# Eight slots of split weights at eight distances past a multiple of 512 bytes: a two-layer encoder on one Trainium2 core

## The chip, the cores and the metric

The kernel runs on one core of a Trainium2 chip. The metric is the device time of one execution in microseconds; the time of the kernel before is the median of two runs, 1114.08 us (1114.03 to 1114.13). The engines of the core go by their short names: PE (TensorE, matmuls; its weight loads are shown apart as PEld), DVE (VectorE), ACT (ScalarE), POOL (GpSimd) and SP (SyncE, which here only issues transfers).

## The reference

A trunk of two layers on an input of 512 tokens by 1024 features, in float32.

- Layer 0: RMSNorm, one projection from 1024 to 2304 columns, split between a short gated convolution (512 wide) and a sliding-window attention (8 query heads, 2 key heads, window 128, ALiBi, a learned sink per head); a norm for each half, one output projection of 1024 by 1024, residual.
- Layer 1: RMSNorm, one projection from 1024 to 1696 columns, split between a spatial gating unit and a latent attention (low-rank queries and keys, a shared rotary key, 8 heads, causal by chunks of 64); norms, an output projection, residual.
- After the mixer of each layer: RMSNorm, a SwiGLU feed-forward of 2816 hidden columns, residual:

```python
h = rmsnorm(x, ffn_norm[layer])
gate, up = jnp.split(h @ w_ffn_in[layer], 2, axis=-1)
x = x + (jax.nn.silu(gate) * up) @ w_ffn_out[layer]
```

## The kernel before, in words

Almost all of the work is products of float32 weights with float32 activations. PE takes them in the format float32r, which keeps fewer bits, so each operand is split: a high part (the value rounded to float32r) and a low part (the value minus its high part, rounded again). Each product is three matmuls that add up in the same stretch of PSUM: high by high, high by low and low by high (`product`, lines 1681 to 1685). The activations are held feature by feature: 128 features on the partitions, 512 tokens along the row.

The weights come in 188 loads. A load is up to 1024 float32 values on each of the 128 partitions (two blocks of 128 input features by 512 columns). It passes three tiles:

1. SP issues the transfer into one of the two slots of `raw`, once the low part of the load two before is made.
2. ACT writes the high part into one of the four slots of `w_hi` (`hi`, line 697), once PE has used the load four before.
3. DVE subtracts and writes the low part into one of the four slots of `w_lo` (`lo`, line 1122).

PE waits for the low part (`ready`) and then works through the load: 2 blocks by 4 tiles of 128 columns, each a product of three matmuls, 24 in all for a full load; load n takes slot n modulo 4. In most stages the 128 by 128 tile of the weights is what PE holds (the stationary operand, fetched by a weight load ahead of every matmul) and the 512 tokens of the activation stream past. In the last feed-forward product (`token_out`), in the value part of the spatial gating unit and in the values of the latent attention it is the other way round: a tile of the activation is held and up to 512 columns of the weights stream past. In the rows of the trace the name that streams stands first and the one that is held second: `ps<-h_hi,w_hi` has `w_hi` held, `ps<-w_hi,act_hi` has it streaming.

The addresses are set by hand. A helper `sb` gives out room on each partition from the bottom up, `place[0]` being the next free byte, which begins at a multiple of 1024. Ahead of the weights stand `xT` (16 KiB), `h_hi` and `h_lo` (16 KiB each) and `raw` (8 KiB); then come `w_hi` and `w_lo`, 16 KiB each, in slots of 4096 bytes. So every slot, every tile of 128 columns in it (512 bytes) and every tile of `h_hi` and `h_lo` begins at a multiple of 512 bytes. Behind the weights come the small tensors: `small` (identity, ones and averaging matrices), `tables`, `gains`, `mix0_gain`, `join`, `gate_bias`, `sinks`, `eps_col`, `spare`, `sel` and `tiny`, 13,376 bytes in all. Then `place[0]` is rounded up to a multiple of 1024, and `row_scale`, `acc`, the scratch tiles and the large region of the activations (`act_hi`, `act_lo` and what shares their room) follow.

The order of the instructions on each engine is written out in the program. No cost table or planner stands behind it. The feed-forward stages are loops on the engines, with all addresses of the weight slots fixed numbers in the loop's body.

Of the kernel before, what the change touches and what calls it, by code (L numbers as in the profile page):

```python
# [16 lines left out]
F32 = mybir.dt.float32  # L17
F32R = mybir.dt.float32r
# [6 lines left out]
P = 128  # L25
# [13 lines left out]
RAW_SLOTS = 2  # L39
W_SLOTS = 4  # L40
LEAD = W_SLOTS


E_Q, E_KV, E_AIN, E_AC, E_AB, E_OUT = 0, 4, 6, 10, 14, 18
# [68 lines left out]
def program(nc, x, mix_norm, ffn_norm, w_ffn_in, w_ffn_out, e_w_in, e_conv, e_q_gain, e_k_gain,  # L113
# [25 lines left out]
    x_blocks = at("x_blocks", [P, QT, DT, 4, 32], F32, h_at + 16 * 1024)  # L139

    raw = sb("raw", [P, RAW_SLOTS, 1024])
    w_hi = sb("w_hi", [P, W_SLOTS, 1024], F32R)
    w_lo = sb("w_lo", [P, W_SLOTS, 1024], F32R)

    small = sb("small", [P, N_SMALL])
    ident, ones = small[:, 0:128], small[:, 128:256]
# [530 lines left out]
    def _(act):  # L677
# [4 lines left out]
        def hi(n, shift=0, count=None):  # L682

            s = n % W_SLOTS
            if n >= W_SLOTS:
                act.wait_ge(load_used, n - W_SLOTS + 1 + shift)
            if count is None:
                act.wait_ge(raw_landed[n % 2], landed(n))
            else:
                act.wait_ge(raw_landed[n % 2], count)  # L690
            if O_CKV <= n < O_CV:
                act.wait_ge(kr_columns, n - O_CKV + 1)
            if n in O_UQ:
                act.wait_ge(uq_columns, O_UQ.index(n) + 1)
            pairs = list(zip(ordered(n, w_hi[:, s, :], None), ordered(n, None, raw[:, n % 2, :])))
            for dst, src in pairs:
                ins = act.activation(dst, src, ACT.Copy)  # L697
            ins.then_inc(hi_done, 1)

        def high_slice(n, k):  # L700

            return act.activation(ordered(n, w_hi[:, n % W_SLOTS, :], None)[k], ordered(n, None, raw[:, n % 2, :])[k],
                                  ACT.Copy)

        def through(p):
# [405 lines left out]
    def _(dve):  # L1111
# [3 lines left out]
        def lo(n, shift=0):  # L1115

            s = n % W_SLOTS
            dve.wait_ge(hi_done, n + 1 + shift)
            parts = zip(ordered(n, w_lo[:, s, :], None), ordered(n, None, raw[:, n % 2, :]),
                        ordered(n, w_hi[:, s, :].bitcast(F32), None))  # L1120
            for dst, src, high in parts:
                ins = TT(dst, src, high, ALU.subtract)  # L1122
            ins.then_inc(lo_done, 1)

        def low_slice(n, k):
            s = n % W_SLOTS
            return TT(ordered(n, w_lo[:, s, :], None)[k], ordered(n, None, raw[:, n % 2, :])[k],
                      ordered(n, w_hi[:, s, :].bitcast(F32), None)[k], ALU.subtract)

        def through(p):  # L1130
            while nxt[0] <= min(p + LEAD, N_LOADS - 1):
# [546 lines left out]
    def _(pe):  # L1678
# [11 lines left out]
        def load(n, tiles, ks, moving, banks, first, last, shift=0, extra=None, before=None):  # L1690

            ready(n, shift)
            hi_, lo_ = w_hi[:, n % W_SLOTS, :], w_lo[:, n % W_SLOTS, :]
            for kk, k in enumerate(ks):
                if kk and extra:
                    extra()
                mh, ml = moving(k)
                th, tl = tiles(hi_, kk), tiles(lo_, kk)  # L1700
                for t, b in enumerate(banks):
                    if before:
                        before(kk, t)
                    ins = product(ps[0:P, b, :], th[t], tl[t], mh, ml,
                                  first and kk == 0, last and kk == len(ks) - 1)
            ins.then_inc(load_used, 1)
# [54 lines left out]

        def first_load():

            def pass_of(kk, left, right, start, stop):
                for t in range(4):
                    c = slice(512 * kk + P * t, 512 * kk + P * t + P)
                    ins = MM(ps[:, t, :], left[:, E_Q % W_SLOTS, c], right[:, kk, :], start=start, stop=stop)
                return ins

            pe.wait_ge(h_hi_ready, 1)  # L1770
            pe.wait_ge(first_high, 1)
            pass_of(0, w_hi, h_hi, True, False)
            pe.wait_ge(h_lo_ready, 1)
            pass_of(0, w_hi, h_lo, False, False)
            pe.wait_ge(first_low, 1)
            pass_of(0, w_lo, h_hi, False, False)
            turn_x(1)
            pe.wait_ge(h_hi_ready, 2)
            pe.wait_ge(hi_done, E_Q + 1)
            pass_of(1, w_hi, h_hi, False, False)  # L1780
            pe.wait_ge(h_lo_ready, 2)
            pass_of(1, w_hi, h_lo, False, False)
            ready(E_Q)
            pass_of(1, w_lo, h_hi, False, False).then_inc(load_used, 1)

        warm_up(3)
        for ft, arrived in ((0, x_first), (1, x_loaded[0])):
# [176 lines left out]
        def ffn_out(layer, bank0, half, extra=None):  # L1964

            c = 22 * layer
            b0 = 4 * ((bank0 + 11 + half) % 2)
            m = FFN_OUT[layer] + 11 * half
            banks = range(b0, b0 + 4)
            A = lambda k: (act_hi[:, k, :], act_lo[:, k, :])  # L1970
            pe.wait_ge(hidden_ready, 1 + c + 20 + 2 * half)
            pe.wait_ge(hidden_lo, c + 20)
            load(m, plain(512, 4), (0, 1), A, banks, True, False)
            if extra:
                extra()
            with pe.Fori(0, 2) as i:
                for j in range(1, 5):
                    ready(m + j, 4 * i)
                    wh, wl = w_hi[:, (m + j) % W_SLOTS, :], w_lo[:, (m + j) % W_SLOTS, :]
                    for kk in range(2):  # L1980
                        k = bass.ds(8 * i + 2 * j + kk, 1)
                        mh = act_hi[:, k, :].rearrange("p k n -> p (k n)")
                        ml = act_lo[:, k, :].rearrange("p k n -> p (k n)")
                        for t in range(4):
                            st = slice(512 * kk + P * t, 512 * kk + P * t + P)
                            ins = product(ps[:, b0 + t, :], wh[:, st], wl[:, st], mh, ml, False, False)
                    ins.then_inc(load_used, 1)
            for j in (9, 10):
                if j == 10:
                    pe.wait_ge(hidden_lo, c + 22)  # L1990
                load(m + j, plain(512, 4), (2 * j, 2 * j + 1), A, banks, False, j == 10)
# [38 lines left out]
        for j in range(4):  # L2030
            n = O_CV + j
            ready(n)
            for kk in range(2):
                if (j, kk) == (1, 0):
                    pe.wait_ge(join_ready, 3)
                    pe.wait_ge(ckv_scaled, 3)
                    MM(ps[:, 5, :], join[:, :], kr[:, 1, :], start=True, stop=True).then_inc(kr_joined, 1)
                if (j, kk) == (1, 1):
                    pe.wait_ge(ckv_summed, 2)
                    mean(M_CKV, 4, ones, acc[:, :])  # L2040
                    pe.wait_ge(ckv_squared, 3)
                    mean(M_KR, 7, ones, sq[:, 0, :])
                if (j, kk) == (3, 1):
                    pe.wait_ge(kr_terms, 2)
                    MM(ps[:, 5, :], turn, kr[:, 0, :], start=True, stop=True).then_inc(kr_added, 1)
                c = slice(512 * kk, 512 * kk + 512)
                for t in range(QT):
                    ins = product(ps[:, t, :], h_hi[:, 2 * j + kk, t * P:(t + 1) * P], h_lo[:, 2 * j + kk, t * P:(t + 1) * P],
                                  w_hi[:, n % W_SLOTS, c], w_lo[:, n % W_SLOTS, c], j == 0 and kk == 0, j == 3 and kk == 1)
            ins.then_inc(load_used, 1)  # L2050
            if j == 2:
                pe.wait_ge(spatial_loaded, 32)
                for b in range(2):
                    if b:
                        pe.wait_ge(rs_step, M_KR + 1)
                    for g in range(4):
                        ins = pe.transpose(ps[:, 6 + b, g * P:(g + 1) * P], w_sp[:, 4 * b + g, :], ident)
                    ins.then_inc(spatial_turned, 1)
# [40 lines left out]
        def key_tiles(half):  # L2099
            n = O_UKV + half  # L2100
            ready(n)
            pe.wait_ge(oq_turned, 6 + 2 * half)
            keys = lambda w, kk, j: w[:, n % W_SLOTS, 512 * kk + P * j:512 * kk + P * j + P]
            for kk in range(2):
                for j in range(2):
                    ins = product(ps[:, 4 + 2 * half + j, :], keys(w_hi, kk, j), keys(w_lo, kk, j),
# [2 lines left out]

        def value_tiles(half, part, bank):  # L2110
            n = O_UKV + half
            values = lambda w, kk: w[:, n % W_SLOTS, 512 * kk + 256:512 * kk + 512]
            for t in (2 * part, 2 * part + 1):
                for kk in range(2):
                    c = 256 * (t % 2)
# [112 lines left out]
        def token_out(half):  # L2228
# [5 lines left out]
                pe.wait_ge(hidden_ready, 1 + 22 + 22)  # L2234

            def slices(n, j, tiles):
                wh, wl = w_hi[:, n % W_SLOTS, :], w_lo[:, n % W_SLOTS, :]
                for kk, t in tiles:
                    k, c, token = 2 * j + kk, slice(512 * kk, 512 * kk + 512), slice(t * P, (t + 1) * P)
                    ins = product(ps[:, b0 + t, :], act_hi[:, k, token], act_lo[:, k, token], wh[:, c], wl[:, c],  # L2240
# [1 line left out]
                return ins  # L2242

            def last_slices(n, t, bank, c0, c1):
                wh, wl = w_hi[:, n % W_SLOTS, :], w_lo[:, n % W_SLOTS, :]
                for kk in range(2):
                    k, c, token = FT - 2 + kk, slice(512 * kk + c0, 512 * kk + c1), slice(t * P, (t + 1) * P)
                    ins = product(ps[:, bank, c0:c1], act_hi[:, k, token], act_lo[:, k, token], wh[:, c], wl[:, c],
# [76 lines left out]
```

## Time and profile before

| what | value |
|---|---|
| median of two runs | 1114.08 us (1114.03 to 1114.13) |
| span of the profiled execution | 1112.0 us from the first to the last instruction |
| what lies around the span | 2.1 us, taken as median less span |
| PE busy | 1102.9 us, 99% of the span, 5105 matmuls |
| PE weight loads busy | 887.1 us, 80%, beside the matmuls |
| DVE / ACT / POOL busy | 560.2 / 420.4 / 102.9 us |
| granted PE clock | 1.0 of full speed over the whole span |
| transfers | 106.00 MB, 95 GB/s on average |

For the profiled execution the page gives the span; the whole-execution time is that of the runs in the first line. A row of the profile names the line of the program, the engine, the operation, and output <- inputs. The length that a row gives for one matmul is from its start to the end of its last write. Matmuls overlap, so what counts for the time is the distance from one start to the next, which the timeline shows.

### The profile page before, as it was taken

Reading aid. Unit: us, or ns where it says so; the run is one execution under the profiler, and the core shown is the slowest. Engines: PE = TensorE matmul, PEld = TensorE weight load, DVE = VectorE, ACT = ScalarE, POOL = GpSimd, SP = SyncE. Lnnn points to the kernel's source line nnn. Section 1 sums busy time; section 2 is a strip of 40 time slices with the busy share of each in tenths; the row PEclk is TensorE's granted clock in tenths of the full one; section 3 lists DMA queues with packets and bytes.
Section 4 is the critical chain, followed back from the end, with each engine's and each line's share of the span. In section 5 each row is a group of like instructions: output and inputs, shape, how many; then the busy total and the mean of one; then the engine's idle time right before and its main releaser. Section 6 shows DMA issues by size and latency. Waiting matters only on the chain. (4 is left out here: it accounts for less than half of the span.)

```text
span 1112.0 us, 13661 instructions
## 1 busy us (share of the span) xinstructions
PE 1102.9 (99%) x5105; PEld 887.1 (80%) x5105; DVE 560.2 (50%) x784; ACT 420.4 (38%) x662; POOL 102.9 (9%) x126
## 2 busy tenths in 40 slices
PE   8999999999999999999999999999999999999998
PEld 7777788888888888888877766788888888888887
DVE  6678977434433433242466588656433433453321
ACT  5545445333322322231345567544322322332110
POOL 6000000001000100000002023000000100110000
PEclk9999999999999999999999999999999999999999
DMA  7422223333333233322233200223233333327431
GB/s 236 159 57 76 76 75 96 114 95 95 94 94 94 94 102 103 98 95 85 67 103 94 77 35 1 77 96 112 89 101 94 94 97 100 102 78 170 113 123 48
DMA packets 101289, 106.00 MB, mean 95 GB/s; under 512 B 26235, under 2 KB 77888, under 8 KB 101120
## 3 DMA queue, kind: packets, MB, share of 16 engines
q1 hardware_dynamic: 83536, 103.04, 29.8%
q10 hardware_dynamic: 16656, 2.10, 1.1%
q8 instruction: 27, 0.44, 0.2%
q0 software_dynamic: 1056, 0.30, 0.1%
q14 instruction: 14, 0.11, 0.0%
HBM read 101.23 MB, written 2.10 MB: 93 GB/s over the span
## 5 line engine op out<-in xcount | busy, mean ns | idle before, releaser
L1122 DVE TENSOR_TENSOR w_lo<-raw,w_hi 128x1024 fp32r<-128x1024 f32 (+2 forms) x192 | 224.6, 1176 | 419.1 <-ACT w_hi L697 416.3
L697 ACT ACTIVATE w_hi<-raw 128x1024 fp32r<-128x1024 f32 (+2 forms) x192 | 194.2, 1017 | 468.7 <-PE ps L1685 438.4
L1683 PE MATMUL ps<-h_hi,w_hi 128*128 128x512 f32 x912 | 359.7, 394 | 1.0 <-DVE h_lo L1146 1.0
L1685 PE MATMUL ps<-h_hi,w_lo 128*128 128x512 f32 x912 | 355.1, 389 | 0.0
L1684 PE MATMUL ps<-h_lo,w_hi 128*128 128x512 f32 x912 | 355.0, 389 | 0.0
L1683 PEld LDWEIGHTS ps<-h_hi,w_hi 128*128 128x128 f32 x912 | 171.3, 188 | 42.9 <-issue 6.7
L1684 PEld LDWEIGHTS ps<-h_lo,w_hi 128*128 128x128 f32 x912 | 171.2, 188 | 36.7 <-issue 1.7
L1685 PEld LDWEIGHTS ps<-h_hi,w_lo 128*128 128x128 f32 x912 | 171.2, 188 | 35.9
L581 POOL TENSOR_TENSOR ffn_t<-ffn_t,row_scale 128x512 f32<-128x512 f32 x40 | 51.0, 1295 | 614.2 <-ACT ffn_t L883 614.2
L1684 PE MATMUL ps<-w_lo,act_hi 128*128 128x512 f32 (+1 forms) x178 | 68.8, 387 | 0.0
L1685 PE MATMUL ps<-w_hi,act_lo 128*128 128x512 f32 (+1 forms) x178 | 68.8, 387 | 0.0
L1683 PE MATMUL ps<-w_hi,act_hi 128*128 128x512 f32 (+1 forms) x178 | 68.8, 387 | 0.0
L1683 PE MATMUL ps<-act_hi,w_hi 128*128 (+1 forms) x176 | 68.5, 389 | 0.0
L1684 PE MATMUL ps<-act_lo,w_hi 128*128 (+1 forms) x176 | 68.5, 389 | 0.0
L1685 PE MATMUL ps<-act_hi,w_lo 128*128 (+1 forms) x176 | 68.5, 389 | 0.0
L1410 DVE TENSOR_TENSOR ffn_t<-ps,ffn_t 128x512 f32<-128x512 f32 x44 | 30.4, 692 | 44.8 <-POOL ffn_t L581 40.7
L886 ACT ACTIVATE act_hi<-ffn_t 128x512 f32 (+1 forms) x44 | 27.8, 633 | 49.3 <-DVE ffn_t L1410 49.3
L883 ACT ACTIVATE ffn_t<-ffn_t 128x512 f32<-128x512 f32 x44 | 27.1, 632 | 39.0 <-DVE ffn_t L1406 39.0
L1683 PEld LDWEIGHTS ps<-w_hi,act_hi 128*128 128x128 f32 x178 | 33.4, 188 | 6.9
L1684 PEld LDWEIGHTS ps<-w_lo,act_hi 128*128 128x128 f32 x178 | 33.4, 188 | 6.8
L1685 PEld LDWEIGHTS ps<-w_hi,act_lo 128*128 128x128 f32 x178 | 33.4, 188 | 6.7
L1683 PEld LDWEIGHTS ps<-act_hi,w_hi 128*128 128x128 f32 x176 | 33.0, 188 | 6.9
(283 smaller groups left out, 1173.4 us busy)
## 6 DMA issues: line engine op xcount, KB each, us to landing
raw<-in_w_ffn_in SPq DMA_DIRECT2D x88, 512.0 KB, 3.5
raw<-in_w_ffn_out SPq DMA_DIRECT2D x44, 512.0 KB, 3.7
raw<-in_e_w_in SPq DMA_DIRECT2D x17, 512.0 KB, 3.7
raw<-in_o_w_in SPq DMA_DIRECT2D x8, 512.0 KB, 3.6
raw<-in_o_w_out SPq DMA_DIRECT2D x8, 512.0 KB, 3.6
raw<-in_e_w_out SPq DMA_DIRECT2D x8, 256.0 KB, 3.9
raw<-in_e_w_out SPq DMA_DIRECT2D x4, 512.0 KB, 4.5
out_tok<-x_blocks ACTq DMA_DIRECT2D x16, 128.0 KB, 2.5
```

Of the source, the lines that this page charges most:

```text
L581: pool.tensor_tensor(ffn_t[:, t, :], ffn_t[:, t, :], row_scale[:, :], ALU.mult).then_inc(silu_scaled, 1)
L697: ins = act.activation(dst, src, ACT.Copy)
L883: act.activation(ffn_t[:, b, :], ffn_t[:, b, :], ACT.Silu).then_inc(silu_done, 1)
L886: act.activation(dst[:, t, :], ffn_t[:, (t0 + t) % 4, :], ACT.Copy).then_inc(hidden_hi, 1)
L1122: ins = TT(dst, src, high, ALU.subtract)
L1410: TT(ffn_t[:, b, :], ps[:, b0 + 2 + t, :], ffn_t[:, b, :], ALU.mult).then_inc(hidden_ready, 1)
L1683: MM(dst, st_hi, mv_hi, start=start, stop=False)
L1684: MM(dst, st_hi, mv_lo, start=False, stop=False)
L1685: return MM(dst, st_lo, mv_hi, start=False, stop=stop)
```

## The change

The two tensors `w_hi` and `w_lo` become eight, one for each slot, each at an address of its own. The slots still follow each other at 4096 bytes, and on top of that each is shifted by its own number of bytes: 0, 32, 64 and 128 for the high slots, 192, 256, 384 and 448 for the low ones. What comes behind the weights begins 448 bytes later. As 13,376 + 448 = 13,824 is rounded up to the same 14,336 as 13,376 is, `row_scale` and everything behind it stay where they were, and so does everything ahead of the weights. `small`, `tables` and `gains` now begin 448 bytes past a multiple of 512. The instructions of all five engines, their order, their sizes and their waits are the same as before, and only addresses differ.

```diff
+HI_PHASE = (0, 32, 64, 128)
+LO_PHASE = (192, 256, 384, 448)
...
     raw = sb("raw", [P, RAW_SLOTS, 1024])
-    w_hi = sb("w_hi", [P, W_SLOTS, 1024], F32R)
-    w_lo = sb("w_lo", [P, W_SLOTS, 1024], F32R)
+    w_at = place[0]
+    w_hi = [at("w_hi_" + "abcd"[i], [P, 1024], F32R, w_at + 4096 * i + HI_PHASE[i]) for i in range(W_SLOTS)]
+    w_lo = [at("w_lo_" + "abcd"[i], [P, 1024], F32R, w_at + 4096 * (W_SLOTS + i) + LO_PHASE[i]) for i in range(W_SLOTS)]
+    place[0] = w_at + 4096 * 2 * W_SLOTS + 448
...
-            hi_, lo_ = w_hi[:, n % W_SLOTS, :], w_lo[:, n % W_SLOTS, :]
+            hi_, lo_ = w_hi[n % W_SLOTS][:, :], w_lo[n % W_SLOTS][:, :]
```

All other lines of the diff turn `w_hi[:, s, ...]` into `w_hi[s][:, ...]` in the same way.

## Rows read from the trace of the kernel before

**Rows 1.** The page: span, busy time and share of each engine, granted clock.
```profile
span 1112.0 us, 13661 instructions
PE 1102.9 (99%) x5105; PEld 887.1 (80%) x5105; DVE 560.2 (50%) x784; ACT 420.4 (38%) x662; POOL 102.9 (9%) x126
PEclk9999999999999999999999999999999999999999
```

**Rows 2.** Busy time by windows: us, then PE busy (instructions), clock, DMA share, GB/s.
```profile
200.00:540.00 340.00, 340.00 (x1501) 1.00 0.30 94
760.00:1100.00 340.00, 340.00 (x1500) 1.00 0.34 102
```

**Rows 3.** The same view, whole span, of line 1683 and of line 1767 alone.
```profile
0.00:1112.00 1112.00, 579.70 (x1474) 276.78 (x1474) 1.00 0.31 95
0.00:1112.00 1112.00, 6.00 (x24) 4.35 (x24) 1.00 0.31 95
```

**Rows 4.** Timeline at 400 us: start, length, engine, line, work. Weights held.
```profile
399.97 0.39 PE L1683 MATMUL ps<-h_hi,w_hi 128*128 128x512 f32 x1
399.97 0.19 PEld L1684 LDWEIGHTS ps<-h_lo,w_hi 128*128 128x128 f32 x1
400.20 0.39 PE L1684 MATMUL ps<-h_lo,w_hi 128*128 128x512 f32 x1
...
402.69 0.39 PE L1683 MATMUL ps<-h_hi,w_hi 128*128 128x512 f32 x1
```

**Rows 5.** Timeline at 655 us: matmuls of 256 columns, weights streaming.
```profile
655.43 0.28 PE L1685 MATMUL ps<-w_hi,ckv_lo 128*128 128x256 f32 x1
...
657.95 0.28 PE L1685 MATMUL ps<-w_hi,ckv_lo 128*128 128x256 f32 x1
```

**Rows 6.** Timeline at 1091 us: matmuls of 512 columns, weights streaming.
```profile
1090.58 0.39 PE L1683 MATMUL ps<-w_hi,act_hi 128*128 128x512 f32 x1
...
1093.30 0.39 PE L1683 MATMUL ps<-w_hi,act_hi 128*128 128x512 f32 x1
```

**Rows 7.** Groups of one line: least/median/greatest length in ns, first and last start.
```profile
L1684 PE MATMUL ps<-h_lo,w_hi x912: 387/389/402, 15.5 to 988.8; 128*128 128x512 f32 x183
L1683 PE MATMUL ps<-w_hi,act_hi x178: 278/389/389, 989.3 to 1108.6; 128*128 128x512 f32 x174, 128*128 128x256 f32 x4
L1683 PEld LDWEIGHTS ps<-w_hi,h_hi x32: 187/188/190, 575.1 to 600.7; 128*128 128x128 f32 x32
L1683 PEld LDWEIGHTS ps<-w_hi,ckv_hi x16: 186/189/192, 655.1 to 665.5; 128*128 128x128 f32 x16
L2166 PE MATMUL ps<-small,o_p x80: 272/273/332, 669.0 to 704.2; 128*128 128x128 f32 x80
```

**Rows 8.** Groups by line: busy us, mean ns, idle before and its releaser.
```profile
L1122 DVE TENSOR_TENSOR w_lo<-raw,w_hi 128x1024 fp32r<-128x1024 f32 x170 | 207.9, 1226 | 389.0 <-ACT w_hi L697 386.2
L697 ACT ACTIVATE w_hi<-raw 128x1024 fp32r<-128x1024 f32 x170 | 179.3, 1057 | 430.8 <-PE ps L1685 406.0 <-DMA raw<-in_w_ffn_out 7.8 <-issue 7.8
L1684 PE MATMUL ps<-h_lo,w_hi 128*128 128x512 f32 x912 | 355.0, 389 | 0.0
L1685 PE MATMUL ps<-h_hi,w_lo 128*128 128x512 f32 x912 | 355.1, 389 | 0.0
```

**Rows 9.** What PE waited for: us in total, times, longest.
```profile
PE ps L2152 <- ACT o_p L1054: 2.5, 4, 1.0
PE ps L1734 <- DVE warm L1210: 1.9, 1, 1.9
PE ps L1683 <- DVE h_lo L1146: 1.0, 1, 1.0
```

**Rows 10.** The first load of `small`: its issue, its landing, its first reader.
```profile
0.74 0.40 SPq L405 DMA_DIRECT2D small<-const_small  x1
small<-const_small SPq DMA_DIRECT2D x1, 64.0 KB, 1.9
3.92 0.18 PEld L1740 LDWEIGHTS ps<-small,mix_rows 8*128 8x128 f32 x1 [0.65 <-issue]
```

More of the change, by code:

```diff
@@ L694, in hi @@
                 act.wait_ge(uq_columns, O_UQ.index(n) + 1)
-            pairs = list(zip(ordered(n, w_hi[:, s, :], None), ordered(n, None, raw[:, n % 2, :])))
+            pairs = list(zip(ordered(n, w_hi[s][:, :], None), ordered(n, None, raw[:, n % 2, :])))
             for dst, src in pairs:
@@ L700, in high_slice @@
         def high_slice(n, k):
-            return act.activation(ordered(n, w_hi[:, n % W_SLOTS, :], None)[k], ordered(n, None, raw[:, n % 2, :])[k],
+            return act.activation(ordered(n, w_hi[n % W_SLOTS][:, :], None)[k], ordered(n, None, raw[:, n % 2, :])[k],
                                   ACT.Copy)
@@ L1118, in lo @@
             dve.wait_ge(hi_done, n + 1 + shift)
-            parts = zip(ordered(n, w_lo[:, s, :], None), ordered(n, None, raw[:, n % 2, :]),
-                        ordered(n, w_hi[:, s, :].bitcast(F32), None))
+            parts = zip(ordered(n, w_lo[s][:, :], None), ordered(n, None, raw[:, n % 2, :]),
+                        ordered(n, w_hi[s][:, :].bitcast(F32), None))
             for dst, src, high in parts:
@@ L1126, in low_slice @@
             s = n % W_SLOTS
-            return TT(ordered(n, w_lo[:, s, :], None)[k], ordered(n, None, raw[:, n % 2, :])[k],
-                      ordered(n, w_hi[:, s, :].bitcast(F32), None)[k], ALU.subtract)
+            return TT(ordered(n, w_lo[s][:, :], None)[k], ordered(n, None, raw[:, n % 2, :])[k],
+                      ordered(n, w_hi[s][:, :].bitcast(F32), None)[k], ALU.subtract)
         def through(p):
@@ L1762, in first_load @@
         def first_load():
+            weights_high, weights_low = w_hi[E_Q % W_SLOTS], w_lo[E_Q % W_SLOTS]
             def pass_of(kk, left, right, start, stop):
@@ L1766, in pass_of @@
                     c = slice(512 * kk + P * t, 512 * kk + P * t + P)
-                    ins = MM(ps[:, t, :], left[:, E_Q % W_SLOTS, c], right[:, kk, :], start=start, stop=stop)
+                    ins = MM(ps[:, t, :], left[:, c], right[:, kk, :], start=start, stop=stop)
                 return ins
@@ L1771, in first_load @@
             pe.wait_ge(first_high, 1)
-            pass_of(0, w_hi, h_hi, True, False)
+            pass_of(0, weights_high, h_hi, True, False)
             pe.wait_ge(h_lo_ready, 1)
-            pass_of(0, w_hi, h_lo, False, False)
+            pass_of(0, weights_high, h_lo, False, False)
             pe.wait_ge(first_low, 1)
-            pass_of(0, w_lo, h_hi, False, False)
+            pass_of(0, weights_low, h_hi, False, False)
             turn_x(1)
@@ L1779, in first_load @@
             pe.wait_ge(hi_done, E_Q + 1)
-            pass_of(1, w_hi, h_hi, False, False)
+            pass_of(1, weights_high, h_hi, False, False)
             pe.wait_ge(h_lo_ready, 2)
-            pass_of(1, w_hi, h_lo, False, False)
+            pass_of(1, weights_high, h_lo, False, False)
             ready(E_Q)
-            pass_of(1, w_lo, h_hi, False, False).then_inc(load_used, 1)
+            pass_of(1, weights_low, h_hi, False, False).then_inc(load_used, 1)
         warm_up(3)
@@ L1978, in ffn_out @@
                     ready(m + j, 4 * i)
-                    wh, wl = w_hi[:, (m + j) % W_SLOTS, :], w_lo[:, (m + j) % W_SLOTS, :]
+                    wh, wl = w_hi[(m + j) % W_SLOTS][:, :], w_lo[(m + j) % W_SLOTS][:, :]
                     for kk in range(2):
@@ L2048, in _ @@
                     ins = product(ps[:, t, :], h_hi[:, 2 * j + kk, t * P:(t + 1) * P], h_lo[:, 2 * j + kk, t * P:(t + 1) * P],
-                                  w_hi[:, n % W_SLOTS, c], w_lo[:, n % W_SLOTS, c], j == 0 and kk == 0, j == 3 and kk == 1)
+                                  w_hi[n % W_SLOTS][:, c], w_lo[n % W_SLOTS][:, c], j == 0 and kk == 0, j == 3 and kk == 1)
             ins.then_inc(load_used, 1)
@@ L2102, in key_tiles @@
             pe.wait_ge(oq_turned, 6 + 2 * half)
-            keys = lambda w, kk, j: w[:, n % W_SLOTS, 512 * kk + P * j:512 * kk + P * j + P]
+            keys = lambda w, kk, j: w[n % W_SLOTS][:, 512 * kk + P * j:512 * kk + P * j + P]
             for kk in range(2):
@@ L2111, in value_tiles @@
             n = O_UKV + half
-            values = lambda w, kk: w[:, n % W_SLOTS, 512 * kk + 256:512 * kk + 512]
+            values = lambda w, kk: w[n % W_SLOTS][:, 512 * kk + 256:512 * kk + 512]
             for t in (2 * part, 2 * part + 1):
@@ L2236, in slices @@
             def slices(n, j, tiles):
-                wh, wl = w_hi[:, n % W_SLOTS, :], w_lo[:, n % W_SLOTS, :]
+                wh, wl = w_hi[n % W_SLOTS][:, :], w_lo[n % W_SLOTS][:, :]
                 for kk, t in tiles:
@@ L2244, in last_slices @@
             def last_slices(n, t, bank, c0, c1):
-                wh, wl = w_hi[:, n % W_SLOTS, :], w_lo[:, n % W_SLOTS, :]
+                wh, wl = w_hi[n % W_SLOTS][:, :], w_lo[n % W_SLOTS][:, :]
                 for kk in range(2):
```

## The prediction

> **What bounds the kernel now.** I read the page's list of engines first: PE is busy for 1102.9 of 1112.0 us at the full granted clock, and DVE and ACT for half of it or less [rows 1]. The list of PE's waits then says that it hardly waits: its longest entries are 2.5, 1.9 and 1.0 us [rows 9]. The windows show the two long feed-forward stretches without a gap, 340.00 us busy out of 340.00, twice [rows 2]. So the time is the number of matmuls times the distance from one start to the next, and a change of addresses matters only if it changes that distance, or if it slows something so much that PE comes to wait.
>
> The distance comes from the timeline. With the weights held, 12 matmuls take 402.69 - 399.97 = 2.72 us, 226.7 ns each [rows 4]; with the weights streaming, 12 take 1093.30 - 1090.58 = 2.72 us, the same [rows 6]. The windows agree: 680 us over 3001 matmuls is 226.6 ns [rows 2]. Matmuls of 256 columns stand 657.95 - 655.43 = 2.52 us over 21 apart, 120.0 ns [rows 5]. Going from 256 to 512 columns costs 106.7 ns, 0.417 ns a column, which is one column per cycle at 2.4 GHz. 512 columns are 213.3 ns, and **13.3 ns** remain for each matmul, at 512 columns and at 256 alike. That surcharge is the only thing in PE's stream that another address could take away, and the whole question is whether it has to do with addresses.
>
> How many matmuls the change touches: 1474 in each of the three lines of `product`, and 24 in the first load [rows 3], 3 x 1474 + 24 = 4446 of 5105. Weights stream in 178 + 32 + 16 = 226 of the triples (the streaming groups of 178, 32 and 16 in line 1683 [rows 7]), and are held in the other 1482 - 226 = 1256. In a triple two matmuls read the high part and one the low part. One high slot of four keeps its old phase and all the low ones lose it, so 2 x 3/4 + 1 = 2.5 matmuls of a triple are moved: 3140 with weights held, 565 with weights streaming.
>
> **The change, part by part.**
>
> *Held weights.* A tile of 128 columns is 512 bytes and filled one block of 512 exactly; shifted, it lies across a boundary of two. If the weight load takes longer for it, that lies beside the running matmul: a load begins together with a matmul (399.97 both) and the next matmul starts 226.7 ns later [rows 4]. At 256 columns the loads follow each other every 120.0 ns [rows 5], so a load occupies its path for no more than 120.0 ns, though its row says 188 to 189 from start to end [rows 7]. The slack is at least 106.7 ns. Bounds: 0 if that slack covers it; from above, a load doubled to 240.0 ns, 13.3 ns over the distance now, times 3140 = 41.8 us (the second rival). I take 0, since nothing in the rows shows a load near the distance.
>
> *Streaming weights.* 2048 bytes that lay in four blocks of 512 now touch five. Bounds: 0, and the largest lengthening that a row shows for a matmul in this stream, 402 - 389 = 13 ns [rows 7], times 565 = 7.3 us. I take one column's time, 0.4 ns, 0.2 us in all, because the streaming form of the last stage never exceeded 389 ns [rows 7] and one more block in a stream is nearer to one slot of the stream than to thirty.
>
> *Collisions with other engines.* ACT and DVE write the slots while PE reads others. If another address removed every disturbance, the gain is bounded by what the rows show above the undisturbed 389 ns: 355.0 - 912 x 0.389 = 0.2 us and 355.1 - 354.8 = 0.3 us for two of the three large groups [rows 8], and perhaps as much again in the small stages. I take 0 and keep 1.5 us for the range.
>
> *ACT and DVE.* A split of a load takes 1057 and 1226 ns [rows 8] in a period of 24 x 226.7 = 5441 ns. Even at twice their length they would end within the period, and four slots stand between them and PE. ACT spent 406.0 us waiting for PE in these 170 loads alone [rows 8]. Cost 0. With that cover gone a tenth more on each of 170 loads would be 170 x 0.23 = 39 us; it would take a slowing by a factor above 2 to get there.
>
> *What lies behind the weights.* `small` is an operand of many of the other 5105 - 4446 = 659 matmuls; the 80 transposes with it have a median of 273 ns [rows 7]. Bounds 0 and, from the 13 ns above for all of them, 659 x 13 = 8.6 us. I take 0. The first transfer into `small` is issued at 0.74 us, lands in 1.9, at 2.64, and is first read at 3.92 [rows 10]; 1.28 us of slack cover a slower landing. The Trainium skill ("DMA: Bandwidth & Descriptors", how a descriptor splits into AXI transactions) says that a descriptor off a multiple of 256 bytes costs an extra partial transaction. That speaks against the change. By that page the 512 bytes a partition become three transactions in place of two, and even half of 1.9 us more would stay inside the slack, so the sum is the same by it.
>
> *Sum.* 1112.0 us of span + 0.2 + 2.1 around it = 1114.3 us; against the profile's own execution the forecast is no change. The two runs lie at 1114.03 and 1114.13, so a fifth of a microsecond can't be told from them and I say **1114.1 us**.
>
> **The rivals.**
>
> *A, the surcharge is a collision of PE's two readers.* The weight load and the running matmul read at the same time, and before the change both begin at a multiple of 512 bytes. If they get in each other's way on the bits below 512, other phases could take the 13.3 ns away: 4446 x 13.3 = 59.1 us, 1055 us. For it: the surcharge is the same at 512 and 256 columns, as the weight load is. Against it: the streaming operand runs over 512 bytes in 53.3 ns, four times during one matmul, and the weight load passes over the same 512 bytes once, in up to 120 ns. Wherever they start, they pass each other. Also the tiles of a load begin at four different multiples of 512, and all matmuls of the stretch keep the same distance [rows 4]. A fifth of it would be 12 us, 1102 us; 22.3 us (2%) need 38% of it. The Trainium skill ("TensorE: Matmul & The Clock Gate", "Wait — 56ns, not 53.3ns?") gives about 2.5 ns as the fixed cost of a warm matmul; by that rule 10.8 of the 13.3 ns would be avoidable, 48 us, 1066 us. The trace shows 13.3 in every stage and no matmul of this format at 2.5, so the rule doesn't hold for this stream. The same page (Part 2) says that the two have independent read ports, and "SBUF — State Buffer" (two separate sides) that PE never waits for another engine's access. Both speak against A and against B, and no row here contradicts them. Chances: 0.03 for over 38% of the surcharge, 0.03 for a smaller part that shows.
>
> *B, slower: the weight load gets longer than the distance.* Seven of eight slots now have tiles across a boundary of 512 bytes. If a load across one is done as two, its occupancy goes from up to 120.0 to up to 240.0 ns, the matmuls with held weights come every 240.0 instead of 226.7, and the time is 1114.1 + 41.8 = 1156 us. It decides from an occupancy of 226.7 ns on; 2% is passed at 226.7 + 22.3/3140 = 233.8 ns. Against it: the load must nearly double, and the words of a shifted tile are as contiguous as before. Chance 0.02.
>
> *C, a small loss.* Streams and `small` pay several nanoseconds each: up to 7.3 + 8.6 = 15.9 us, 1130 us. Chance 0.04.
>
> *D, the change doesn't do what it says.* It does set eight phases, but the high slot of every fourth load keeps phase 0, and what it is read against (`h_hi`, `act_hi`) stays at 0 as well. Under A a quarter of the high matmuls would keep their surcharge. That alters A's size and not my forecast.
>
> **How the numbers follow.** No change has 0.88, and its value is 1114.1 us. Its own range: 1.5 us less without disturbances, 1.5 more from the ends of the small terms, 1112.5 to 1115.6. For 8 in 10 I add half a microsecond on the side of the small gains and a microsecond on that of the small losses: **1112.0 to 1116.5 us**. What is left out is A (0.06), B (0.02) and most of C (0.04), 0.12. Over 2% faster (under 1091.8) is A's first part, 0.03; over 2% slower (above 1136.4) is B, 0.02; within 2%, about what a measurement of this kernel tells from no change, is 0.95.
>
> **What would show it.** In the changed kernel's timeline at 400 and 1091 us, 12 matmuls should again take 2.72 us in each slot, high or low. Under A the loads of slots 1 to 3 would be closer together than those of slot 0, and the windows of 340 us would hold more than 1501 matmuls. Under B the form with held weights would be further apart and the streaming form not. Under C the medians of 389 or 272 ns would rise. ACT's wait for PE at line 697 should stay near 406 us. I am wrong if the distance depends on a slot's phase at all, or if DVE's 1226 ns changes by enough for PE to wait for `w_lo`.

## The result: 19.4 us slower

The changed kernel takes 1133.49 us (median of 2, 1133.24 to 1133.73) where the kernel before took 1114.08. The ratio is 1.0174 with a 95% interval of 1.015 to 1.0199. I had forecast 1114.1 us, no change, with a range that ended at 1116.5.

The page of the changed kernel, with the same rows as [rows 1]:

```profile
span 1131.4 us, 13661 instructions
PE 1122.4 (99%) x5105; PEld 888.1 (78%) x5105; DVE 560.2 (50%) x784; ACT 420.4 (37%) x662; POOL 103.3 (9%) x126
PEclk9999999999999999999999999999999999999999
```

The span grew by 19.4 us and PE's busy time by 19.5. DVE and ACT have the same busy time to the tenth, POOL and the weight loads differ by 0.4 and 1.0 us, and the clock is the same. So no other engine accounts for it, and PE takes longer for as many matmuls. Its waits are those of [rows 9], to the tenth:

```profile
PE ps L2158 <- ACT o_p L1058: 2.5, 4, 1.0
PE ps L1738 <- DVE warm L1214: 1.9, 1, 1.9
PE ps L1687 <- DVE h_lo L1150: 1.0, 1, 1.0
```

The busy time by windows, PE alone, answers to [rows 2]:

```profile
200.00:540.00 340.00, 340.00 (x1469) 1.00 0.31 94
760.00:1100.00 340.00, 340.00 (x1469) 1.00 0.36 101
```

680 us now hold 2938 matmuls in place of 3001, 231.5 ns each in place of 226.6. PE is as dense as before and each matmul is 4.9 ns further from the next; 4446 x 4.9 = 21.8 us is more than the 19.4 measured. Both traces hold all 5105 matmuls in the same order, so each can be set beside its twin: the matmuls with weights held grew by 17.0 us in all, those with weights streaming by 2.3 and the other 659 by 0.1. With weights held it is 4.9 ns each in the two long stretches and 3.6 ns between 27.8 and 200 us.

The timeline of line 1687, which was 1683 before, shows the first matmul of each load. I show one round of the four slots, 96 matmuls:

```profile
402.67 0.40 PE L1687 MATMUL ps<-h_hi,w_hi_b 128*128 128x512 f32 x1
...
408.23 0.39 PE L1687 MATMUL ps<-h_hi,w_hi_c 128*128 128x512 f32 x1
...
413.78 0.40 PE L1687 MATMUL ps<-h_hi,w_hi_d 128*128 128x512 f32 x1
...
419.36 0.40 PE L1687 MATMUL ps<-h_hi,w_hi_a 128*128 128x512 f32 x1
...
424.90 0.40 PE L1687 MATMUL ps<-h_hi,w_hi_b 128*128 128x512 f32 x1
```

A load of 24 matmuls takes 5.56, 5.55, 5.58 and 5.54 us in slots b, c, d and a, where it took 2 x 2.72 = 5.44 before [rows 4]. Slot a is as slow as the others although its high part stayed at phase 0. Last, the lengths of one matmul and of one weight load, as in [rows 7]:

```profile
L1688 PEld LDWEIGHTS ps<-h_lo,w_hi_b x234: 187/188/192, 15.4 to 1005.9; 128*128 128x128 f32 x117
L1688 PE MATMUL ps<-h_lo,w_hi_b x234: 387/393/403, 15.6 to 1006.1; 128*128 128x512 f32 x117
```

The weight load still takes 188 ns. What has grown is the matmul, from a median of 389 to 393 ns. That speaks against rival B, a longer weight load, and fits two readers that meet while the matmul streams.

Matmuls of 256 columns, as in [rows 5], pay nothing. In slot a, where the high part streams at phase 0 and the low part at 192:

```profile
666.98 0.28 PE L1687 MATMUL ps<-w_hi_a,ckv_hi 128*128 128x256 f32 x1
...
669.11 0.28 PE L1687 MATMUL ps<-w_hi_a,ckv_hi 128*128 128x256 f32 x1
```

These are 18 matmuls in 2.13 us, 118.3 ns each, where it was 120.0; in slot b, from 671.88 to 673.06 us, ten take 1.18 us, 118 ns each. The cost is in the matmuls of 512 columns.

### The profile page after: what moved, and what is told of

Same layout as the page of the kernel before. It is cut to its first block, busy times and chain, and to the rows that moved or that the text cites. A ratio compares the mean times of both kernels' runs of the same rounds, so it can differ in the third digit from the quotient of the medians.

```text
span 1131.4 us, 13661 instructions
## 1 busy us (share of the span) xinstructions
PE 1122.4 (99%) x5105; PEld 888.1 (78%) x5105; DVE 560.2 (50%) x784; ACT 420.4 (37%) x662; POOL 103.3 (9%) x126
## 4 chain that ended last, share of the span: by engine, by line
PE 95%; DVE 3%; ACT 1%; DMA 1%; issue 0%; SPq 0%; ACTq 0%
PE ps L1687 30%; PE ps L1689 30%; PE ps L1688 29%; PE ps L1720 1%; PE ps L1845 1%; PE ps L2185 1%; DVE tiny L1584 0%; DVE o_p L1604 0%; ACT o_p L1058 0%; PE ps L2172 0%; DVE e_pT L1304 0%; PE ps L1867 0%; PE ps L2158 0%; DMA x_tok<-in_x 0%; PE ps L1855 0%; DMA raw<-in_e_w_in 0%
## 5 line engine op out<-in xcount | busy, mean ns | idle before, releaser
L1687 PE MATMUL ps<-h_hi,w_hi_b 128*128 128x512 f32 x234 | 93.0, 397 | 1.0 <-DVE h_lo L1150 1.0
L1689 PE MATMUL ps<-h_hi,w_lo_b 128*128 128x512 f32 x234 | 92.4, 395 | 0.0
L1688 PE MATMUL ps<-h_lo,w_hi_b 128*128 128x512 f32 x234 | 92.0, 393 | 0.0
L1687 PE MATMUL ps<-h_hi,w_hi_c 128*128 128x512 f32 x226 | 90.9, 402 | 0.0
L1687 PE MATMUL ps<-h_hi,w_hi_d 128*128 128x512 f32 x226 | 90.6, 401 | 0.0
L1687 PE MATMUL ps<-h_hi,w_hi_a 128*128 128x512 f32 x226 | 90.0, 398 | 0.0
L1689 PE MATMUL ps<-h_hi,w_lo_a 128*128 128x512 f32 x226 | 89.2, 395 | 0.0
L1689 PE MATMUL ps<-h_hi,w_lo_d 128*128 128x512 f32 x226 | 89.1, 394 | 0.0
L1688 PE MATMUL ps<-h_lo,w_hi_a 128*128 128x512 f32 x226 | 89.0, 394 | 0.0
L1688 PE MATMUL ps<-h_lo,w_hi_d 128*128 128x512 f32 x226 | 88.9, 393 | 0.0
```

The lines of the kernel that those rows point to most:

```text
L1687: MM(dst, st_hi, mv_hi, start=start, stop=False)
L1688: MM(dst, st_hi, mv_lo, start=False, stop=False)
L1689: return MM(dst, st_lo, mv_hi, start=False, stop=stop)
```

## The experiments

The phase of an operand is its start address modulo 512, and the address offset of a pair is the phase of the held tile less that of the streaming operand. Four theories stood at the start. **T1**: an operand off a multiple of 512 bytes costs by itself. **T2**: the address offset between the held tile and the streaming operand counts. **T3**: what costs is that consecutive weight loads begin at different phases. **T4**: the cost is in what lies behind the weights.

### One held tile against one streaming operand

```diff
+HELD = tuple(32 * i for i in range(16))
+FLOW = (0, 64, 192, 256)
+REPEAT = 36
...
+    return [(h, f) for f in range(len(FLOW)) for h in range(len(HELD)) for _ in range(REPEAT)]
```

> Leaves the encoder out and measures the disputed cost alone: one held tile of 128 columns against one streaming operand of 512 columns, 36 matmuls for each of 16 phases of the held tile (0 to 480 by 32 bytes) and 4 phases of the streaming operand (0, 64, 192, 256). T1, absolute alignment: a held tile that begins off a multiple of 512 bytes costs by itself; 226.7 ns at phase 0 in all four quarters, some 230 to 236 ns at all 15 others, whatever the streaming phase. T2, relative phase: only the distance between held and streaming counts; 226.7 ns on the diagonal (0/0, 64/64, 192/192, 256/256) and the curve of each quarter is the first one moved by the streaming phase. T3, change of address from load to load: a held tile that stays the same keeps 226.7 ns at every phase, in all 64 pairs.

Each row of the timeline is a run of 36 matmuls; `held_a` to `held_p` are the phases 0 to 480 by 32, `flow_a` is phase 0 and `flow_b` phase 64. The distance between two starts is the difference of two rows' starts over 36:

```profile
29.26 8.56 PE L74 MATMUL ps<-flow_a,held_c 128*128 128x512 f32 x36
37.66 8.59 PE L74 MATMUL ps<-flow_a,held_d 128*128 128x512 f32 x36
...
62.85 8.40 PE L74 MATMUL ps<-flow_a,held_g 128*128 128x512 f32 x36
71.08 8.56 PE L74 MATMUL ps<-flow_a,held_h 128*128 128x512 f32 x36
79.48 8.33 PE L74 MATMUL ps<-flow_a,held_i 128*128 128x512 f32 x36
87.65 8.55 PE L74 MATMUL ps<-flow_a,held_j 128*128 128x512 f32 x36
...
162.92 8.33 PE L74 MATMUL ps<-flow_b,held_c 128*128 128x512 f32 x36
171.09 4.12 PE L74 MATMUL ps<-flow_b,held_d 128*128 128x512 f32 x17
...
213.07 8.40 PE L74 MATMUL ps<-flow_b,held_i 128*128 128x512 f32 x36
221.31 8.56 PE L74 MATMUL ps<-flow_b,held_j 128*128 128x512 f32 x36
```

`held_c` (64) costs 8.40 us a run against `flow_a` (0) and 8.17 against `flow_b` (64): 233.3 and 226.9 ns. `held_i` (256) does the reverse: 8.17 against `flow_a` and 8.24 against `flow_b`. Taken from the 13th to the last matmul of each run, the means by address offset (held minus streaming, modulo 256) are the same to 0.1 ns in all four quarters, but for the pair 0/0, which came first and began with matmuls 427 ns apart:

| address offset, bytes | 0 | 32 | 64 | 96 | 128 | 160 | 192 | 224 |
|---|---|---|---|---|---|---|---|---|
| ns from start to start | 226.7 | 233.4 | 233.4 | 234.1 | 232.7 | 233.1 | 228.8 | 233.3 |

T2 holds, with a period of 256 bytes. T1 falls: 64 against 64 and 192 against 192 are both off 512 and cost nothing. T3 falls as a full account: a tile that never changes pays 6.7 ns at 32 or 64. What the runs show is this dependence on the offset; how the two accesses hold each other up inside the chip they don't show.

### The triple of the kernel

```diff
+HELD = tuple(64 * i for i in range(8))
...
+    return [(t, f) for lo in range(8) for hi in range(8) for _ in range(REPEAT) for t, f in ((hi, 0), (hi, 1), (lo, 0))]
```

> Leaves the encoder out: the triple of the kernel (a high tile twice, a low tile once, both streaming operands at phase 0) 12 times for each of 8 high phases and 8 low phases (0 to 448 by 64). T1: with high and low both off 0 the triple is longer than 680 ns, and a phase is as bad as high or low; 0/0 gives 680 ns. T2: the same here, since the streaming phase is 0 in all. T3: the diagonal (high phase equal to low phase) gives 680 ns everywhere and the other 56 are longer, up to some 700 ns.

The pattern repeats every 256 bytes here too. The means in ns a matmul, from the fifth triple on and good to 0.2 ns (0/0 itself came first and was still settling, so its value is that of 0/256, 256/0 and 256/256):

| low phase \ high phase | 0 | 64 | 128 | 192 |
|---|---|---|---|---|
| 0 | 226.7 | 233.3 | 233.3 | 228.9 |
| 64 | 231.1 | 233.3 | 230.0 | 228.9 |
| 128 | 231.2 | 231.1 | 232.1 | 233.5 |
| 192 | 231.1 | 231.9 | 233.5 | 228.9 |

The diagonal isn't free, so T3 is out. The costs of the high and the low tile don't add: a low tile off 0 beside a high one at 0 costs 4.4 ns on every matmul of the triple, and with the high tile at 64 or 192 the low tile's phase may cost nothing more, or give something back (64 with 128: 230.0 against 233.3).

### Only what lies behind the weights

```diff
-HI_PHASE = (0, 32, 64, 128)
-LO_PHASE = (192, 256, 384, 448)
+HI_PHASE = (0, 0, 0, 0)
+LO_PHASE = (0, 0, 0, 0)
```

> All eight slots back at phase 0 as eight tensors; only what lies behind the weights stays 448 bytes later. T1, T2 and T3 (the cost is in the matmuls with the split weights): 1114 us, ratio 1.000. T4 (small, tables and gains off their boundary, or the split into eight tensors, carry the cost): 1133 us, ratio 1.017.

1113.99 us against 1113.99 before, ratio 1.000 (0.999 to 1.0009). T4 is out: neither the eight tensors nor `small` and `tables` at 448 cost anything.

### All eight slots at phase 192

```diff
-HI_PHASE = (0, 32, 64, 128)
-LO_PHASE = (192, 256, 384, 448)
+HI_PHASE = (192, 192, 192, 192)
+LO_PHASE = (192, 192, 192, 192)
```

> All eight slots at the same phase, 192, activations still at 0. T1 (absolute alignment) and T2 (distance to the streaming operand): slower than before, some 1130 to 1140 us, ratio 1.015 to 1.025, since now every load is off. T3 (the weight loads of a triple begin at different phases): 1114 us, ratio 1.000.

1125.51 us, ratio 1.0104 (1.0087 to 1.0121). Slower, as T1 and T2 had it, but by less than I wrote. The timeline shows why: first a load with weights held, then one with weights streaming:

```profile
404.37 0.39 PE L1687 MATMUL ps<-h_hi,w_hi_c 128*128 128x512 f32 x1
...
409.87 0.39 PE L1687 MATMUL ps<-h_hi,w_hi_d 128*128 128x512 f32 x1
...
1059.15 0.39 PE L1687 MATMUL ps<-w_hi_b,act_hi 128*128 128x512 f32 x1
...
1064.75 0.39 PE L1687 MATMUL ps<-w_hi_c,act_hi 128*128 128x512 f32 x1
```

Held weights at 192 past the stream: 5.50/24 = 229.2 ns. Streaming weights, where the held tile is 192 short of the stream, so an offset of 64 modulo 256: 5.60/24 = 233.3 ns. The table of pairs has 228.8 and 233.4. One phase of the same tensor costs 2 or 7 ns, by which side it is on. An absolute alignment could do that only with a price of its own for each side; the next run leaves no room for it.

### Everything shifted together

```diff
-    base = (nc.sbuf_base + 1023) // 1024 * 1024
+    base = (nc.sbuf_base + 1023) // 1024 * 1024 + 192
...
-    place[0] = (place[0] + 1023) // 1024 * 1024
+    place[0] = (place[0] - 192 + 1023) // 1024 * 1024 + 192
```

> The kernel before with every tensor, activations and all, 192 bytes later: each address is off 512, each distance between two operands is as before. T1 (absolute alignment): at least as slow as the changed kernel, 1133 us or more. T2 (relative phase): 1114 us, ratio 1.000.

1114.16 us against 1113.93, ratio 1.000 (0.9991 to 1.001). Every operand of the products is off 512 and nothing is lost. In the windows PE does what it did before:

```profile
200.00:540.00 340.00, 340.00 (x1501) 1.00 0.31 95
760.00:1100.00 340.00, 340.00 (x1500) 1.00 0.36 102
```

### Only the high slots, only the low slots

```diff
 HI_PHASE = (0, 32, 64, 128)
-LO_PHASE = (192, 256, 384, 448)
+LO_PHASE = (512, 512, 512, 512)
...
-    place[0] = w_at + 4096 * 2 * W_SLOTS + 448
+    place[0] = w_at + 4096 * 2 * W_SLOTS + 512
```

> Only the high slots at 0, 32, 64, 128; the low ones at phase 0. T2 with the table of pairs and triples: held weights 0, 6.7, 6.6 and 6.6 ns a matmul in the four slots, 5.0 on average x 3768 = 18.7 us, streaming weights 1.7 us, together 20 us: 1133 us, ratio 1.017 to 1.018. A cost that adds up from the slots moved (high and low alike, 3 of 7): 1122 us.

1131.21 us, ratio 1.0156 (1.0139 to 1.0173). The expectation of 1133 us was 2 us high, its ratio of 1.017 at the edge of the interval; the sum over slots moved (1122) is far off. One round of the four slots shows where the tables were too high:

```profile
401.85 0.39 PE L1687 MATMUL ps<-h_hi,w_hi_b 128*128 128x512 f32 x1
...
407.40 0.39 PE L1687 MATMUL ps<-h_hi,w_hi_c 128*128 128x512 f32 x1
...
412.96 0.40 PE L1687 MATMUL ps<-h_hi,w_hi_d 128*128 128x512 f32 x1
...
418.56 0.39 PE L1687 MATMUL ps<-h_hi,w_hi_a 128*128 128x512 f32 x1
...
424.01 0.39 PE L1687 MATMUL ps<-h_hi,w_hi_b 128*128 128x512 f32 x1
```

Slots b, c and d take 5.55, 5.56 and 5.60 us for a load, slot a 5.45. Slot d has its 6.6 ns a matmul; b and c lose some 5 where 6.7 and 6.6 were expected. The round of 96 matmuls takes 22.16 us, 230.8 ns each.

```diff
-HI_PHASE = (0, 32, 64, 128)
+HI_PHASE = (0, 0, 0, 0)
 LO_PHASE = (192, 256, 384, 448)
...
-    place[0] = w_at + 4096 * 2 * W_SLOTS + 448
+    place[0] = w_at + 4096 * 2 * W_SLOTS + 512
```

> Only the low slots at 192, 256, 384, 448; the high ones at phase 0. T2 with the table: 4.4, 0, 4.5 and 4.4 ns in the four slots, 3.3 x 3768 = 12.5 us, streaming 1.1 us, together some 13 us: 1127 us, ratio 1.012; slot b (256) keeps 226.7 ns. A cost that adds up from the slots moved (4 of 7): 1125 us, with slot b as slow as the others.

1127.35 us, ratio 1.0119 (1.0102 to 1.0135), as the tables had it. The first matmul of each load again:

```profile
400.86 0.39 PE L1687 MATMUL ps<-h_hi,w_hi_b 128*128 128x512 f32 x1
...
406.30 0.39 PE L1687 MATMUL ps<-h_hi,w_hi_c 128*128 128x512 f32 x1
...
411.84 0.39 PE L1687 MATMUL ps<-h_hi,w_hi_d 128*128 128x512 f32 x1
...
417.39 0.39 PE L1687 MATMUL ps<-h_hi,w_hi_a 128*128 128x512 f32 x1
```

Slot b, whose low part lies at 256, takes 5.44 us for its load, the old time; slots c and d take 5.54 and 5.55. The two parts cost 17.3 and 13.4 us, and both together, in the changed kernel, 19.4.

### Eight slots at multiples of 256

```diff
-HI_PHASE = (0, 32, 64, 128)
-LO_PHASE = (192, 256, 384, 448)
+HI_PHASE = (0, 256, 256, 512)
+LO_PHASE = (512, 512, 768, 768)
...
-    place[0] = w_at + 4096 * 2 * W_SLOTS + 448
+    place[0] = w_at + 4096 * 2 * W_SLOTS + 768
```

> High slots at 0, 256, 256, 512 and low slots at 512, 512, 768, 768, all multiples of 256: four of the eight lie 256 past a multiple of 512. T2 with a period of 256 bytes, as the table of pairs has it: 1114 us, ratio 1.000. A period of 512 bytes (the table's repeat being chance): four slots off, some 1120 to 1130 us.

1113.88 us against 1113.62, ratio 1.0001 (0.9991 to 1.001). The period of 256 bytes holds in the whole kernel.

### Is there a phase better than 0?

```diff
+    return [(0, 0, 0)] * REPEAT + [(h, 0, k) for h in range(8) for k in range(8) for _ in range(REPEAT)]
...
+            ins = MM(ps[:, b, 0:S], held[h][:, k:k + P], flow[f][:, :], start=n < 12 and n % 3 == 0, stop=n > last - 12 and n % 3 == 2)
```

> Leaves the encoder out: one held tile of 128 columns at 64 phases from 0 to 252 bytes by steps of 4, the streaming operand at phase 0, 36 matmuls each. T2, with lines of 32 bytes or more as its unit: steps, 226.7 ns from 0 to 28, some 233 ns after it, 228.8 from 192 to 220. T2 with a finer unit: a smooth or toothed curve between the values known at multiples of 32 (226.7, 233.4, 233.4, 234.1, 232.7, 233.1, 228.8, 233.3). If a phase between them lies under 226.7 ns, a kernel faster than the one before could be built on it; I expect none.

The phases between multiples of 32 are those of 128 columns taken from a wider tile, k columns in. Run m3_fine, the same sweep with a tensor of its own for each phase, gave no result. The 64 means, again from the 13th matmul on, run from 226.7 to 237.8 ns with no order that I can read: 0, 4, 8, 12 and 16 bytes give 226.7, 232.4, 230.7, 230.3 and 233.3, and 156 and 164 bytes give 226.7 and 237.8. There are no steps of 32 bytes. Seven of the 64 phases lie at 226.7 and none under it. Single intervals go down to 224 ns, but always with longer ones in the same round.

### Are the remaining 13.3 ns a collision as well?

```diff
+HELD = (0, 64, 192)
+WIDTHS = (128, 96, 64, 32)
...
+    return [(0, 128)] * REPEAT + [(h, w) for w in WIDTHS for h in range(3) for _ in range(REPEAT)]
```

> Leaves the encoder out: held tiles of 128, 96, 64 and 32 columns at phases 0, 64 and 192, the streaming operand of 512 columns at phase 0, 36 matmuls each. T5, the 13.3 ns that stay at the best phase are themselves reads of the weight load that hold up the stream: they shrink with the columns loaded, 226.7, 223.3, 220.0 and 216.7 ns at phase 0, and what phase 64 adds (6.6 ns) shrinks as well. T6, they are a fixed cost of changing the held tile: 226.7 ns at phase 0 for every width, and only what phases 64 and 192 add (6.6 and 2.1 ns) shrinks.

```profile
40.66 8.44 PE L75 MATMUL ps<-flow_a,held_a 128*96 128x512 f32 x36
48.94 8.39 PE L75 MATMUL ps<-flow_a,held_b 128*96 128x512 f32 x36
57.17 8.56 PE L75 MATMUL ps<-flow_a,held_c 128*96 128x512 f32 x36
...
90.44 8.50 PE L75 MATMUL ps<-flow_a,held_a 128*32 128x512 f32 x36
98.78 8.50 PE L75 MATMUL ps<-flow_a,held_b 128*32 128x512 f32 x36
107.12 8.50 PE L75 MATMUL ps<-flow_a,held_c 128*32 128x512 f32 x36
```

Both expectations fail. At phase 0 a narrower held tile is slower, not faster: 8.28/36 = 230.0 ns with 96 columns and 8.34/36 = 231.7 with 32, against 226.7 with 128. At phase 64 it is the other way round: 8.23/36 = 228.6 ns with 96 columns, against 233.4 with 128. With 32 columns phases 0, 64 and 192 all give 231.7. So the 13.3 ns don't shrink with the columns loaded, as reads that each cost a slot would; and the 226.7 ns are no fixed base either. Width and phase together decide where between 226.7 and some 234 ns a stream settles. What it is inside PE that settles there stays open.

## Why the prediction was wrong

**The step that failed** is the part "Held weights", where I took 0. I asked whether the weight load gets longer, and found slack for it. Both were right: the load stays at 188 ns. But I priced only that. The other cost, the load holding up the stream beside it, I had only as rival A, and only as a gain. There the sentence that failed is "Wherever they start, they pass each other". The table of pairs shows that where they start decides 0 to 7 ns of each matmul. The four tiles of a load are 512 bytes apart, so the equal distances of [rows 4], which I took as evidence, are equal phases and say nothing of other offsets.

The trace before had a sign that I overlooked. "The trace shows 13.3 in every stage" holds only where the stream has settled. Here it resumes after two matmuls with `small`, and every operand of the products is at a multiple of 512:

```profile
760.97 0.40 PE L1684 MATMUL ps<-h_lo,w_hi 128*128 128x512 f32 x1
...
763.04 0.39 PE L1684 MATMUL ps<-h_lo,w_hi 128*128 128x512 f32 x1
...
765.08 0.39 PE L1684 MATMUL ps<-h_lo,w_hi 128*128 128x512 f32 x1
```

The first nine distances take 2.07 us, 230.0 ns each, the next nine 2.04 us, 226.7 ns. The single intervals run from 224 to 236 ns, and other such breaks in this trace are followed by the same. So the distance wasn't fixed even with all phases equal. That this settling and the cost of an offset have one cause is likely but not shown.

**The sign.** Rival A, two readers of PE that meet by their address bits, comes nearest to what the runs show, and its direction was reversed. It took the 13.3 ns for a collision that another phase could remove. At 512 columns they are what stays at the best phase found, and every other multiple of 32 within the 256 adds to them. A forecast with an unpriced term should have kept both signs of it: I had a gain of up to 59.1 us and no loss from the same cause. The rows bound neither, and the 0.03 for a visible part of A had no twin on the slow side.

**Streaming weights** were taken at 0.2 us. In the last stage with all slots at phase 192 the distance is 233.3 in place of 226.7 ns. In the changed kernel the table of pairs gives, for the high slots at offsets 0, 224, 192 and 128 and the low ones at 64, 0, 128 and 64, a mean of 4.1 ns, 678 x 4.1 = 2.8 us; the traces side by side have 2.3. I had counted only the 565 shifted ones at 0.4 ns.

**Held weights, sized by the runs.** The round of the four slots above is 22.23/96 = 231.6 ns, 4.9 over 226.7; 3768 x 4.9 = 18.5 us. With 2.8 that is 21.3 us, where 19.4 were measured. From the tables in the same way the sum is 12.8 for the one-phase kernel (11.5 measured), 20.4 for the high slots alone (17.3) and 13.6 for the low ones alone (13.4). It runs up to a fifth too high. One reason is that it gives the settled rate to every matmul: between 27.8 and 200 us, where breaks are frequent, the changed kernel lost 3.6 ns a matmul and not 4.9. With the high slots alone the round above loses 4.2 ns a matmul in place of 5.0, so the tables themselves don't carry over exactly to slots b and c, and why stays open.

**The rest held.** ACT and DVE kept their lengths (1226 ns before; the page's busy times are equal), collisions with them gave nothing, and `small` behind the weights cost nothing (ratio 1.000). Rival B, the weight load done as two at a boundary of 512, is refuted by the kernel with everything shifted: its tiles lie across such boundaries and it lost nothing. Rival C, several nanoseconds for each streaming operand, 1130 us, was near in size, but by a cost of its own for each operand off 512, which the kernel with everything shifted rules out. Rival D is refuted in its detail: slot a, high part at phase 0, paid 231 ns like the others, as the low part's phase spreads over the triple. The low end of no change's own range is 1114.1 - 1.5 = 1112.6 and not 1112.5; nothing hangs on it.

Of the two pages of the Trainium skill that I set against A and B, the one on SBUF speaks of other engines' accesses and has no bearing on two readers of PE. The other, the Trainium skill's "TensorE: Matmul & The Clock Gate" (Part 2), says that PE's two read ports are independent and that loading the next tile doesn't take read bandwidth from the running matmul. Here 6.7 ns of 226.7 go to just that pair of accesses, by their offset alone, so for float32r at 512 columns the measurement decides against it, as far as it says that the two don't disturb each other. The 2.5 ns that the same page gives as the fixed cost of a warm matmul were not reached by any settled stream here; the least is 13.3 ns at 512 columns and, in the changed kernel, 118.3 - 106.7 = 11.6 ns at 256.

## What to carry to other kernels

Where PE streams float32r matmuls of 512 columns, each with a weight load of 128 columns beside it, keep all operands of PE at the same phase modulo 256 bytes; then shifting them together is free (by 192 bytes, in the whole kernel). Moving one of them against the other costs 3% of each matmul at most multiples of 32 and 5% at the worst phase seen. Not all matmuls pay: those of 256 columns didn't, nor the 80 float32 transposes with `small` at phase 448, which were busy for 10.41 us before and after. Other formats were not tried. Staggering buffers has to be measured on the pair that PE reads at the same time, and padding of an odd size ahead of a tile is such a stagger. When a trace holds only one value of the quantity that a change varies, its evenness is no evidence that the quantity doesn't matter: leave room on both sides.

## What the runs showed that I had not expected

- The distance from one matmul's start to the next depends on the offset of two addresses: at 512 columns 226.7 ns at 0, 228.8 at 192, 232.7 to 234.1 at the other multiples of 32, with a period of 256 bytes.
- In finer steps there is no visible order: 226.7 ns at 156 bytes and 237.8 at 164.
- The matmuls fall into short repeating rounds: at offset 64 the intervals alternate 236 and 231 ns, at 192 they go 226, 229, 232.
- A narrower held tile doesn't help at offset 0: with 32 columns the matmuls stand 231.7 ns apart, with 128 at 226.7.
- With 256 streaming columns the offsets of the changed kernel cost nothing: 118.3 ns against 120.0.
